# A two-layer mixture-of-experts encoder: expert weights loaded in transfers of four chunks instead of two

## The reference

```python
def expert_choice_moe(x, w_router, b_router, w_gate, w_up, w_down):
    b, s, d = x.shape
    cap = EC_CAPACITY_FACTOR * s // N_EXPERTS
    logits = (x @ w_router).astype(jnp.float32) + b_router.astype(jnp.float32)
    aff = jax.nn.softmax(logits, axis=-1)
    gates, idx = lax.top_k(aff.transpose(0, 2, 1), cap)
    xs = jax.vmap(lambda xb, ib: xb[ib])(x, idx)
    hid = jax.nn.silu(jnp.einsum('becd,edf->becf', xs, w_gate)) * jnp.einsum('becd,edf->becf', xs, w_up)
    o = jnp.einsum('becf,efd->becd', hid, w_down) * gates[..., None].astype(x.dtype)
    y = jax.vmap(lambda ib, ob: jnp.zeros((s, d), ob.dtype).at[ib.reshape(-1)].add(ob.reshape(-1, d)))(idx, o)
    return y

    for l in range(DEPTH):
        ...
        x = layer_norm(DEEPNORM_ALPHA * x + mix, ln1_g[l], ln1_b[l])
        moe = expert_choice_moe(x, w_router[l], b_router[l], w_gate[l], w_up[l], w_down[l])
        x = layer_norm(DEEPNORM_ALPHA * x + moe, ln2_g[l], ln2_b[l])
```

## Time and profile before

| | us |
|---|---|
| median of 3 runs | 1618.17 (1606.86 to 1623.52) |
| the profiled execution, its own time | 1613.03 |
| its span | 1611.2 |
| TensorE busy | 1406.9 (87%) |
| VectorE, ScalarE, GpSimd busy | 519.3, 299.0, 231.5 |
| DMA traffic | 462.64 MB, 432.62 MB of it on the ring's queue |
| expert weights | 192 transfers of 2048 KB |

### The profile page before, as it was taken

The page is one execution under the profiler, slowest core; times in us unless marked ns, Lnnn a source line. Parts: engine busy times, 40 slices in busy tenths (PEclk is TensorE's granted clock), DMA queues, the critical chain, the costliest instruction groups (busy, mean ns, idle before and its releaser), DMA issues.

```text
span 1611.2 us, 14886 instructions
## 1 busy us (share of the span) xinstructions
PE 1406.9 (87%) x6044; PEld 703.1 (44%) x6044; DVE 519.3 (32%) x937; ACT 299.0 (19%) x523; POOL 231.5 (14%) x162
## 2 busy tenths in 40 slices
PE   4998799889999889889689978996999999889893
PEld 4874357533333333333268734684333333233231
DVE  4573863511101101101449457445011101101105
ACT  3234550100000000000132245401100000000000
POOL 2443510000000000000145444011000000000003
PEclk9998579889999999999979975997999999999997
DMA  8411002689999999999780200118999999999992
GB/s 345 164 53 52 1 1 79 253 352 428 428 428 427 427 427 427 428 428 428 281 309 24 105 0 1 53 40 342 395 428 427 427 427 428 427 428 427 428 428 84
DMA packets 42483, 462.64 MB, mean 287 GB/s; under 512 B 6704, under 2 KB 7344, under 8 KB 14000
## 3 DMA queue, kind: packets, MB, share of 16 engines
q1 hardware_dynamic: 31968, 432.62, 63.9%
q0 software_dynamic: 4032, 14.68, 2.5%
q10 hardware_dynamic: 6416, 14.39, 2.4%
HBM read 451.18 MB, written 10.49 MB: 287 GB/s over the span
## 4 chain that ended last, share of the span: by engine, by line
PE 63%; DMA 19%; DVE 8%; issue 4%; ACT 2%; POOL 2%; POOLq 1%; DVEq 0%; SPq 0%; ACTq 0%
DMA ring<-w_moe 19%; PE bank L758 17%; PE bank L447 11%; PE bank L781 10%; PE bank L736 7%; PE bank L595 2%; PE bank L692 2%; PE bank L693 2%; PE bank L694 2%; PE bank L411 1%; DVE stat L1009 1%; PE bank L524 1%; PE bank L583 1%; PE bank L635 1%; PE bank L715 1%
## 5 line engine op out<-in xcount | busy, mean ns | idle before, releaser
L758 PE MATMUL bank<-ring,work 128*64 128x512 f32 x2048 | 447.8, 594 | 32.6 <-DMA ring<-w_moe 20.8
L758 PEld LDWEIGHTS bank<-ring,work 128*64 128x64 f32 x2048 | 167.8, 137 | 302.4 <-issue 246.3
L781 PE MATMUL bank<-ring,work 128*64 128x512 f32 x1024 | 231.2, 597 | 29.5 <-DMA ring<-w_moe 17.7
L1184 DVE TENSOR_TENSOR X<-X,bank 128x512 f32<-128x512 f32 x128 | 87.8, 686 | 315.6 <-PE bank L736 315.4
L1172 DVE TENSOR_TENSOR work<-work,bank 128x512 f32<-128x512 f32 x32 | 22.0, 688 | 494.1 <-PE bank L758 492.6
L781 PEld LDWEIGHTS bank<-ring,work 128*64 128x64 f32 x1024 | 77.0, 136 | 171.5 <-issue 143.9
L736 PE MATMUL bank<-work 128*128 128x512 f32 x256 | 125.5, 620 | 13.1 <-ACT work L1435 11.2
L1424 ACT ACTIVATE work<-bank 128x512 f32<-128x512 f32 x64 | 38.0, 598 | 354.2 <-PE bank L411 354.2
L1548 POOL COPY cur<-slot_i 128x1 int32<-128x1 int32 x16 | 2.9, 184 | 607.2 <-PE bank L411 550.0
L1485 POOL TENSOR_TENSOR w_lo<-ring,w_hi 128x2048 fp32r<-128x2048 f32 x16 | 73.6, 4602 | 110.1 <-ACT w_hi L1233 79.5
L447 PE MATMUL bank<-x_hi,w_hi 128*128 128x512 f32 x288 | 77.0, 412 | 11.7 <-POOL w_lo L1485 5.9
(11 more groups left out here) (196 smaller groups left out, 1446.4 us busy)
## 6 DMA issues: line engine op xcount, KB each, us to landing
ring<-w_moe SPq DMA_DIRECT2D x192, 2048.0 KB, 29.0
ring<-w_in SPq DMA_DIRECT2D x18, 1024.0 KB, 12.7
ring<-w_out SPq DMA_DIRECT2D x8, 1024.0 KB, 23.0
out<-X POOLq DMA_DIRECT2D x12, 512.0 KB, 5.7
X<-out ACTq DMA_DIRECT2D x2, 2048.0 KB, 8.6
x_rows<-X ACTq DMA_DIRECT2D x8, 512.0 KB, 2.7
X<-x_in ACTq DMA_DIRECT2D x4, 512.0 KB, 7.9
ring<-ln SPq DMA_DIRECT2D x2, 1024.0 KB, 6.8
```

The costliest lines, as they stand in the source:

```text
L758: ins = mm(B((kind, pair, n))[64 * e:64 * e + 64, :], xsT[:, k, 64 * e:64 * e + 64], w[:, e, n * 512:(n + 1) * 512], start=(k == 0), stop= ...
L781: ins = mm(B(("O", pair, n))[64 * e:64 * e + 64, :], hidT[:, k, 64 * e:64 * e + 64], w[:, i, e], start=(k == 0), stop=(k == KD - 1))
L1184: nc.vector.tensor_tensor(X[:, t, cols], X[:, t, cols], B(name)[:, :], ALU.add)\
```

## The change

JOINED goes from 2 to 4. Everything else follows from that constant: a transfer of expert weights carries four neighbouring chunks, 4 MiB with 32 KiB contiguous per partition on both sides; there are 48 transfers in a layer instead of 96; the host lays `w_moe` out accordingly; SP waits for four free slots before each; and a reader of any of the four chunks waits for the landing of all four. The ring keeps its 16 slots, and the four groups of slots are 4 to 7, 8 to 11, 12 to 15 and 0 to 3. The groups fall together with A to F. No instruction of a compute engine changes.

```diff
--- before.py
+++ after.py
@@ -68,7 +68,7 @@
 CHUNKS = -(-USED // RING) * RING
 
 
-JOINED = 2
+JOINED = 4
 assert MOE_AT % JOINED == 0 and PAIR_CHUNKS % JOINED == 0
```

## The result

| | before | joined by four |
|---|---|---|
| median, us | 1614.08 (17 runs) | 1623.57 (17 runs) |
| ratio to before | 1 | 1.0051, 95% interval 1.0037 to 1.0065 |
| profiled execution, us | 1613.03 | 1620.21 |
| its span, us | 1611.2 | 1618.4 |

What follows compares the result with a forecast made beforehand. The DMA weight stream was taken as the bound of the expert stage. Restart and end add 7.1 us a layer, less 0.9 for the rate: +13.3 us, 1631 us against the 1618.2 median; own range 1619 to 1640, 8-in-10 range 1613 to 1646.

Steps and rivals of the forecast that it cites:

- what bounds the kernel: Expert stage, from the fourth pair on: it runs at the pace of the DMA engines, 58.8 us a pair plus gathers.
- the end: Last F of each layer: its first matmul waits for all four chunks, 4.8 us later in layer 0, 4.9 in layer 1.
- the restart: First refill of the full ring waits for four free chunks: stream late by 2.3 us in layer 0, 2.2 in layer 1.
- the prediction's upper bound: First refill in each layer: the whole stream late by 3.4 us, the full delay of its issue.
- The step that took 1.1 us off: First refill: delay below 3.4 us, since the earlier first transfer shared the engines with a gather's tail, which will be past.
- the term of the rate: Both layers' weight streams of 434 us: larger rows save 0.1%, 0.9 us, bounds 0 and 8.7.
- the choice between the bounds: Rate of the two streams: 0.1% taken, near the low end, because 428 GB/s looked like a ceiling.
- The upper bound: Rate of the two streams: doubling the packet again saves 12.5 ns in 1230, 1.0%, 8.7 us.
- the 25 ns of the first doubling: Weight queue: two 8 KiB packets take 0.640 us against 0.615 for one of 16 KiB, at most 25 ns saved.
- the clock: Matmuls behind TensorE's longer waits: a granted clock below 1.00 would show the forecast wrong; no time in the sum.
- Is never late: TensorE in the steady stage: waits some 2.5 us each before E and F, and always keeps up with the stream.

Runs made afterwards that it cites:

- the best version: Joined kernel with first refill as 1, 1, 2 chunks, two-chunk transfers from the last pair but one's E on, last F as 1, 1, 2: ratio 0.9944 to before.

## Why the prediction was right and wrong

**Right: what bounds the kernel.** In the joined kernel and the kernel before, the stream of expert weights sets the stage's end: F's first matmuls start right at a landing. Where TensorE had more work (four unread matmuls) or the end was made finer, TensorE ran the last part at its own pace, behind an earlier landing.

**Right: the end.** Forecast 4.8 and 4.9 us; F starts 780.02 - 332.76 = 447.3 and 1578.63 - 1131.37 = 447.3 us after the stage's start, before 442.6 and 442.3: +4.7 and +5.0. The experiment with the last F alone joined gives 4.7 for layer 0.

**Too small: the restart.** Issue and time to landing of the first refill of the joined kernel, layer 0 and layer 1:

```profile
L391 SPq DMA_DIRECT2D ring<-w_moe x1: 328/328/328, 340.7 to 340.7; - x1
...
DMA to landing us min/median/max: 13.6/13.6/13.6
...
L391 SPq DMA_DIRECT2D ring<-w_moe x1: 327/327/327, 1139.3 to 1139.3; - x1
...
DMA to landing us min/median/max: 12.2/12.2/12.2
```

It goes out 7.9 us after the stage's start, as forecast, and lands at 21.5 and 20.1, where the second small one landed at 18.2 and 18.4: +3.3 and +1.7, in sum 5.0 against 4.5. In layer 0 the transfer took 13.6 us, not 12.6. But the small figure of layer 1 does not last. The refill that ends eight chunks later, layer 0 of the kernel before and of the one with rows of 16 KiB, where no rate is gained:

```profile
L391 SPq DMA_DIRECT2D ring<-w_moe x1: 327/327/327, 359.0 to 359.0; - x1
...
DMA to landing us min/median/max: 16.1/16.1/16.1
...
L391 SPq DMA_DIRECT2D ring<-w_moe x1: 368/368/368, 356.0 to 356.0; - x1
...
DMA to landing us min/median/max: 19.5/19.5/19.5
```

Counted from the stage's start it lands some 3.3 us later, in layer 1 3.1, and at the last landing the difference is still 3.1 and 3.3. So the restart costs 3.2 us a layer, 6.4 in sum: nearly all of the 3.4 us by which the first refill goes out later, the prediction's upper bound. The step that took 1.1 us off (a gather's tail "will be past") did not hold. Splitting the refill gave back only 1.2 us at the last landing. Its second part landed 2.7 and 1.5 us earlier than the joined refill; the rest went in single longer intervals of the stream, whose cause no run isolates.

**Wrong: the term of the rate.** The sum took 0.9 us, 0.1%, for the larger rows. The step that failed is the choice between the bounds: "428 GB/s is held so evenly over both plateaus that it looks like a ceiling". An even rate with one packet size says nothing of another size. Measured: 13 ns a packet, 6.5 us at the last landings of two layers (3.3 and 3.2, against rows of 16 KiB), about 5.6 us more than the term. The upper bound, 12.5 ns and 8.7 us, was close to this by luck. It halved the 25 ns of the first doubling, but at each doubling two packets become one, so a fixed cost of 25 ns would have been saved whole again, 2.0%, some 17 us. What saved it is that 0.320 us for an 8 KiB packet came from a queue that was not full; in a full one it takes 0.314, and the first doubling saves 13 ns as well. Together with the restart, the faster stream makes the last landing of each layer the same as before within 0.2 us (447.1 and 447.1 us, before 447.3 and 447.0). Only the end was left of the price.

**Wrong: the clock.** The prediction named a halved clock behind TensorE's longer waits as a sign of error, but priced it at nothing. It was there: 1.7 us in one of the two layers, in each of two profiles.

**Not foreseen: how far the end reaches back.** "Is never late" held for the joined kernel, by 2.6 us before the last F in layer 0 and 1.9 in layer 1. It did not hold once its end was made finer: the wait for 4 MiB in the pair before is passed on through a pair of 54.5 us.

**The sum by the stages:** restart 6.4 (forecast 4.5), end 9.7 (9.7), clock 1.7 (0), rate -6.5 (-0.9): 11.3 us against 13.3. That it came so near is luck in part: three terms were off, by 1.9, 1.7 and -5.6 us, and in part they cancel. The ratio gives 8.2 us (6.0 to 10.5), the medians 9.5. For ten of the twelve other kernels the stages' difference lies within the interval of the ratio; for the joined kernel itself it is 3 us above the ratio's 8.2, and this stays open. The rest of the span, outside the two stages, runs from 704.8 to 714.0 us over all profiles, and differs by 4 us between the two of the kernel before. As for the absolute time, the forecast of 1631 stood on a median of three runs, 1618.2, that came down to 1614.1 with 17.

## What to carry to other kernels

When a stream of transfers sets the pace, the middle wants large rows and the ends want small transfers: the first refill is delayed by the slots it waits for, and the consumer's first matmul by all the bytes that land with it. The fine end must begin early enough, here more than one pair of 54.5 us before the end, since a consumer that is nearly as slow as the stream does not catch up; in the best version a transfer of 4 MiB, read two pairs before the last one, still set the end. And when two bounds of a price are worked out from rows, an even rate is no reason to take the lower one.

## What the hardware showed that I had not expected

- A packet of SP's queue costs 12 to 13 ns beside its bytes, from 8 to 32 KiB: 0.314, 0.615 and 1.218 us. From 16 to 32 KiB the rate from 500 to 700 us rises from 427 to 431 GB/s.
- The granted clock fell to 0.51 behind a wait of 2.60 us for the last F in layer 0 and stayed at 1.00 behind one of 1.94 us in layer 1 of the same run. Over all pairs F's first half was slow behind 13 of 24 such waits, once behind 2.03 us, and not behind one of 2.64. It fell in both layers of the kernel with only the last F joined, behind a wait of 6.18 us in layer 0. With 1.98 us of unread matmuls in the wait F's first half took 3.65 us in all 16 pairs.
- Gathers that share the engines with 32 KiB packets took 16.5 us to land in place of 11.5 in the kernel before, the medians over 500 to 700 us (12.0 with rows of 16 KiB in transfers of 4 MiB, 8.5 with rows of 8 KiB). TensorE waited 0.5 us for them in the whole run.
